# Two attention passes of the differential branch: last block's transposes, reciprocal turns and second pair's first outputs placed behind more products of the next branch

## The reference

```python
def _diff_blocked(q, k, v, lam, scale):
    ...
    def body(qi):                       # 4 blocks of 128 queries
        sc = jnp.einsum('bqkgcd,bskcd->cbkgqs', qi, k).astype(jnp.float32) * scale
        p = jax.nn.softmax(sc, axis=-1)
        w = (p[0] - lam * p[1]).astype(v.dtype)
        return jnp.einsum('bkgqs,bskd->bqkgd', w, v)
...
o_d = (_rmsnorm(o_d, subln_d[l]) * (1.0 - lam_init)).reshape(b, s, NQ_D * 2 * DIFF_DIM)
mix = jnp.concatenate([o_a * jax.nn.silu(g_a), o_b * jax.nn.silu(g_b),
                       o_c * jax.nn.silu(g_c), o_d * jax.nn.silu(g_d)], axis=-1)
x = x + jnp.einsum('bsm,md->bsd', mix, w_out[l])
```

## Time and profile before

| | us |
|---|---|
| median of 3 runs | 1462.36 |
| lowest, highest | 1458.74, 1462.77 |
| the profiled execution, its own time | 1460.76 |
| span of the profiled execution, first to last instruction | 1459.0 |
| TensorE busy in that span | 1398.9 |
| VectorE busy | 851.3 |
| ScalarE busy | 729.0 |
| GpSimd busy | 379.9 |

### The profile page before, as it was taken

How to read it: one execution, slowest core, us unless ns; L and a number is a source line. 1 busy time by engine, 2 the same in 40 slices (tenths; PEclk the granted TensorE clock), 3 DMA queues, 4 the chain that set the end, 5 groups by cost and what they waited for, 6 DMA issues and landing times.

```text
span 1459.0 us, 20170 instructions
## 1 busy us (share of the span) xinstructions
PE 1398.9 (96%) x7530; PEld 1054.9 (72%) x7530; DVE 851.3 (58%) x1505; ACT 729.0 (50%) x1557; POOL 379.9 (26%) x273
## 2 busy tenths in 40 slices
PE   8999999999999999999999899999899999999897
PEld 7867677778787667777777776766667876676666
DVE  4565436367662654364576774548665575558655
ACT  4555447555244554465564364435544464446443
POOL 2232132245231321223464121321102111421001
PEclk9999999999999999999999999999999999999999
DMA  7413451225242131211256523511233341611311
GB/s 234 116 31 92 112 141 29 68 71 224 101 159 59 37 97 51 79 47 50 71 209 195 137 61 71 117 64 51 62 105 87 102 101 29 123 58 51 109 59 58
DMA packets 185894, 135.65 MB, mean 93 GB/s; under 512 B 91334, under 2 KB 166726, under 8 KB 185798
## 3 DMA queue, kind: packets, MB, share of 16 engines
q1 hardware_dynamic: 182022, 120.22, 30.4%
q10 hardware_dynamic: 3776, 14.16, 2.6%
HBM read 122.03 MB, written 12.32 MB: 92 GB/s over the span
## 4 chain that ended last, share of the span: by engine, by line
PE 77%; DVE 12%; ACT 7%; issue 2%; DMA 0%; POOL 0%; ACTq 0%; DVEq 0%; POOLq 0%
PE pb L1576 20%; PE pb L1578 18%; PE pb L1577 18%; PE pb L1598 6%; PE pb L1661 6%; PE pb L1637 4%; ACT prob L1717 3%; ACT tmp L1717 2%; DVE prob L2337 2%; DVE wl L2086 2%; PE pb L1692 1%; ACT wh L1737 1%; PE pb L1609 1%; PE pb L1646 1%; DVE small L2323 1%
## 5 line engine op out<-in xcount | busy, mean ns | idle before, releaser
L2481 POOL TENSOR_TENSOR wl<-wr,wh 128x512 fp32r<-128x512 f32 x178 | 250.7, 1408 | 840.2 <-ACT wh L1737 836.9
L1576 PE MATMUL pb<-xh,wl 128*128 128x512 f32 (+1 forms) x880 | 353.6, 402 | 9.2 <-DVE wl L2086 6.9
L1578 PE MATMUL pb<-xh,wh 128*128 128x512 f32 (+1 forms) x880 | 326.1, 371 | 0.0
L1577 PE MATMUL pb<-xl,wh 128*128 128x512 f32 (+1 forms) x880 | 325.8, 370 | 0.0
L2086 DVE TENSOR_TENSOR wl<-wr,wh 128x512 fp32r<-128x512 f32 x208 | 161.0, 777 | 184.8 <-ACT wh L1737 184.5
L1737 ACT CAST wh<-wr 128x512 fp32r<-128x512 f32 (+1 forms) x386 | 220.4, 606 | 36.8 <-PE pb L1578 17.8
L1576 PEld LDWEIGHTS pb<-xh,wl 128*128 128x128 f32 x880 | 167.8, 191 | 71.2 <-issue 39.8
L1578 PEld LDWEIGHTS pb<-xh,wh 128*128 128x128 f32 x880 | 168.0, 191 | 29.5
L1577 PEld LDWEIGHTS pb<-xl,wh 128*128 128x128 f32 x880 | 168.7, 192 | 22.1 <-issue 3.4
L1717 ACT ACTIVATE prob<-prob,small 128x512 f32<-128x512 f32 (+3 forms) x128 | 76.2, 596 | 119.3 <-DVE small L2300 119.1
L1637 PEld LDWEIGHTS pb<-cst,prob 128*128 128x128 f32 x768 | 91.1, 140 | 50.0 <-issue 30.2
(11 more groups left out here) (198 smaller groups left out, 2350.8 us busy)
## 6 DMA issues: line engine op xcount, KB each, us to landing
wr<-w_in SPq DMA_DIRECT2D x39, 1024.0 KB, 5.4
wr<-w_out SPq DMA_DIRECT2D x14, 1024.0 KB, 5.1
wr<-w_in SPq DMA_DIRECT2D x48, 256.0 KB, 4.5
wr<-w_branch SPq DMA_DIRECT2D x48, 128.0 KB, 2.3
x<-prob SPq DMA_DIRECT2D x12, 512.0 KB, 3.0
wr<-w_mem_kv SPq DMA_DIRECT2D x4, 1024.0 KB, 5.6
prob<-x ACTq DMA_DIRECT2D x2, 2048.0 KB, 11.1
wr<-w_out SPq DMA_DIRECT2D x16, 256.0 KB, 4.2
```

Source lines behind the costliest of these rows:

```text
L1576: e.matmul(ps, ll, rh, start=start, stop=False)
L1577: e.matmul(ps, lh, rl, start=False, stop=False)
L1578: t = e.matmul(ps, lh, rh, start=False, stop=stop)
L2481: t = e.tensor_tensor(wl[:, j % 2, c0:c1], wr[:, j % 2, c0:c1], wh[:, j % 2, c0:c1].bitcast(F32), ALU.subtract)
```

## The change

Three due times are moved, all of them for `D` alone. The reciprocals' turn (`rturn`) of each pair comes 1400 ns of the planner's clock after the last transposes, no longer at once. The first `pv` of the second pair comes 1500 ns later. The transposes of the second pair's last block may come 3500 ns later (10500 after the scores, no longer 7000).

```diff
-FRONTS, FIRST_EXP = 5000, 2800
+FRONTS, FIRST_EXP, LAST_MIX = 5000, 2800, 3500
@@ attention(), back
             if i == 3 and br != "sb":
-                yield 0
+                yield now() + 1400 if br == "D" else 0
                 b = AT.take()
                 put("rturn", l=l, br=br, c=c, b=b, rt=rt[c], u=us[0])
@@ attention(), outputs
             yield copied
             if i == 1:
+                if c and br == "D":
+                    yield now() + 1500
                 ob[c] = OB.take()
@@ attention(), loop over the blocks
-                ready = now() + EXPS.get(br, 4000)
+                ready = now() + EXPS.get(br, 4000) + LAST_MIX * (br == "D" and c == 1 and i == 3)
```

## The result

The changed kernel takes 1466.85 us (median of 7 runs, 1465.52 to 1470.73), the kernel before, beside it, 1461.59 us (7 runs, 1458.74 to 1463.26). The ratio is 1.0042, 95% interval 1.003 to 1.0054: slower by 0.42%; it is the ratio on record and not the quotient of the two medians, which is 1.0036. The forecast was 1467.4 us in a range from 1460.0 to 1472.0.

The account below looks back on a forecast made before the run. TensorE, busy 1398.9 of 1459.0 us, was taken as the bound. Waits gave +0.5 us and clock falls +4.5, together +5.0: 1467.4 us from the median of 1462.36, range 1460.0 to 1472.0.

Parts of the forecast that it names:

- Step 1: The first pair's `rturn` moves behind one more product: an estimated 0.5 us a pass gained, no more.
- Step 2: Second pair's first `pv` and block 3's turns: old waits go, new ones of 1.4 and 2.4 us come; about 0.6 gained.
- E: Start of the first exponential of the second pair's block 3, forecast to come later by some 0.6 us.
- Step 3: Tail and start of `C`: a new 2.8 us wait for VectorE's low part, before the third product behind `C`'s second scores.
- Step 4: In `C`, the 0.54 us wait for a low part that GpSimd delays goes: 0.5 us a pass gained.
- The sum: Both passes without the clock: second pass +1.2 us, first pass -0.7, together +0.5.
- The clock: Behind the long new waits, four places in two passes: three falls to 1.2 GHz at 1.5 us, +4.5 us.
- (a): Rival: the waits come, the clock mostly holds, at most two falls; -0.5 to +3.5 us, about 1463.8; chance 0.27.
- (b): Rival: fill banks free when needed, tail not late, the change wins; up to -12 us, more likely half, 1456; chance 0.12.
- (c): Rival: tail later still, each `dsplit` another us late, a fall at each place; +8 to +10 us, 1471; chance 0.08.

Follow-up runs that it names:

- e1_turn: Kernel before with only the `rturn` edit (1400 later, both pairs): 1459.31 us, ratio 0.9988.
- e10_all_short: Kernel after (all three edits) with 1500 for 3500 in the shift of the second pair's block 3 turns: 1456.76 us, ratio 0.9958 to before.
- e3_mix: Kernel before with only the third edit, the second pair's block 3 turns 3500 later: 1459.67 us, ratio 0.9983.
- e6_turn_mix: Kernel after without the edit of the second pair's first `pv`, so `rturn` and the 3500 shift together: 1468.19 us, ratio 1.0036 to before.
- e5_swap: Kernel after with the copies of `C`'s four value tiles exchanged between ScalarE and VectorE: 1459.56 us, ratio 0.9989 to before.
- e7_turn_mix_short: Kernel before with the `rturn` edit and the block 3 turns shifted by 1500 for 3500, without the `pv` edit: 1456.10 us, ratio 0.9956.
- e12_all_2500: Kernel after (all three edits) with 2500 for 3500 in the shift of block 3's turns: 1458.68 us, ratio 0.9973 to before.
- e2_pv: Kernel before with only the second edit, the second pair's first `pv` 1500 later: 1466.38 us, ratio 1.0025.
- e4_turn_pv: Kernel before with the `rturn` and first `pv` edits, without the shift of block 3's turns: 1464.78 us, ratio 1.0023.
- e9_mix_short: Kernel before with only the third edit, at 1500 for 3500: 1455.63 us, ratio 0.9954.
- e11_short_ahead: e7_turn_mix_short with block 3's mix and reciprocals written out directly behind its scores: 1455.76 us, ratio 0.9955 to before.

## Why the prediction was right, and where it was not

**What bounds the kernel.** Held. In the fourteen kernels a pass differs mostly by what TensorE waits and by the falls; in every pass without a fall its busy time is 98.3 to 99.4 us.

**Step 1, `rturn`, 0.5 us a pass gained.** Not held: from the first marker to block 3's scores the second pass takes 21.61 us before, 21.60 in e1_turn and 21.62 in the kernel after. Nor did it gain further on: e1_turn has 6.41 us of waits where the second pass before has 6.26, since the moved `rturn` pulls a weight piece forward whose GpSimd part lies over `dnewton`. With the clock level in both, e1_turn's pass 2 is 0.52 shorter all the same, all of it busy time.

**Step 2.** Held. E comes 6.55 us behind block 3's scores (1363.21 - 1356.66), 6.09 before: 0.46 where I had 0.6. The keys' bank comes at E + 3.83 (E + 3.7), with a wait of 1.27 (1.4); tile 0's at E + 9.17 (E + 9.2), with 2.21 (2.4). The rule of the Trainium skill, page SBUF — State Buffer, section Who interferes with whom, that VectorE is held up by GpSimd with both its inputs in SBUF and not with one of them in PSUM, is borne out where before only the mixes spoke. GpSimd runs from 1359.88 for 1.29 us, and the instruction of `dnewton` with both inputs in SBUF takes 1.62, 0.69 before. In the second pair's tail GpSimd runs from 1388.23: the instruction with an input in PSUM, beside it nearly all its length, takes 0.68 as alone, and the one behind it, with both in SBUF, 1.14.

```profile
1359.88 1.29 POOL L2483 TENSOR_TENSOR wl<-wr,wh 128x512 fp32r<-128x512 f32 x1 [9.30 <-ACT wh L1739]
1360.10 1.62 DVE L2055 SCALAR_TENSOR_TENSOR scr<-scr,tmp 128x512 f32<-128x512 f32 x1
...
1388.23 1.29 POOL L2483 TENSOR_TENSOR wl<-wr,wh 128x512 fp32r<-128x512 f32 x1 [18.28 <-ACT wh L1739]
1388.21 0.68 DVE L2052 SCALAR_TENSOR_TENSOR scr<-pb,tmp 128x512 f32<-128x512 f32 x1
1388.93 1.14 DVE L2055 SCALAR_TENSOR_TENSOR scr<-scr,tmp 128x512 f32<-128x512 f32 x1
```

**Step 3, the tail.** From the second `pv` (V) to the third product behind `C`'s second scores: V + 17.04 in the first pass after (1071.33 - 1054.29), forecast V + 17.2. e10_all_short has 17.02 and e3_mix 17.09, and the other kernels with a wait there 16.8 to 17.2, but for the second pass of e6_turn_mix with 18.6, where the DMA issues of the last section come in: this chain is about 17 us whatever TensorE does in it. The wait in it was 2.12, forecast 2.8, because TensorE's own work in it is 14.9 us, not 14.4. To the third product, the second pass is longer by 1.2 us once its fall is taken out, where -1.1 + 2.8 = 1.7 was forecast. The first pass is 59.81 us to there, before 60.86: with its own fall only just beginning it is 1.1 shorter, where 0.2 was forecast.

**Step 4 failed.** I took 0.5 us off each pass since the 0.54 in `C` would go, and took the rest of `C` as unchanged. The 0.54 did go, but with 3500 and the other edits the list of `C` itself is another: products have changed places with turns, one of them waits 0.78 for a bank that VectorE's addition (L2426) must free, and from the third product to the second marker TensorE needs 47.9 us (e5_swap, e6_turn_mix, no fall), where it is 46.6 before and 46.7 to 46.8 in e3_mix, e7_turn_mix_short, e10_all_short and e12_all_2500. That is +1.3 a pass where I had -0.5. Of the 1.3, 0.2 is waits; the other 1.1 is busy time with the same instructions. The timelines say where it lies: from start to start, without the waits, the matmuls of the 32 products of this stretch take 23.8 us before and 25.0 in e5_swap, and all else differs by 0.1 in sum. A product's first matmul takes 0.31 to 0.34 us to the next when attention's matmuls stand ahead of it, and mostly 0.22 to 0.24 otherwise, and the order has 30 changes between products and attention where before has 22. But e3_mix and e12_all_2500 have 28, and their products take only 24.2; what else in the order counts stays open.

**The sum.** Without the clock the two stretches are 7.49 - 3 x 1.54 = 2.9 us longer, forecast +0.5; the term that was mis-sized is step 4, by 1.8 us in the second pass and 1.9 in the first, and the stretch up to the third product was 0.5 and 0.9 too dear. **The clock**: three falls of four places at 1.5, forecast and seen, 1.54 measured. The total of +5.0 stands against +5.3 of the medians and +9.1 of the profiled executions. That the number lies so close is luck: the sum without the clock was 2.4 too small, and 2.9 + 4.6 = 7.5 is more than the medians show. How many falls the median run has is not seen in any profile; its granted clock of 0.991, against 0.988 in the profiled execution, speaks for fewer, though falls outside the two passes count in it too. The first pass of before has a fall in its profiled execution; whether in each of its runs, neither.

**The rivals.** (a) had two falls at most and is not what the profile shows. (b) decided, as written, at whether the mix of block 3 ends before TensorE has done tile 1: it did not (the mix ends at 1371.3, tile 1 at 1372.38 - 2.21 = 1370.2). e10_all_short (0.42% faster) and e5_swap (0.11%) show that a win was to be had, by another size or another engine for one copy. (c), each `dsplit` another us late, did not come: 13.5 us behind V where 13.65 was forecast.

## What to carry to other kernels

Moving independent work in front of a wait gained here only where the next wait did not grow by as much. A chain runs from block 3's scores over the mix to the turns, and a second one of 17 us from the last `pv` to the next branch's weights; every product put ahead of the turns is missing behind the `pv`. Count the products on either side against both chains: 15 or 16 between block 3's scores and its turns and 17 to 19 behind the `pv` was right, 21 and 12 (the kernel after) was not, and the size of the shift (1500 or 3500) decided more than whether the other two edits stood beside it. A copy that frees a bank should not stand at the end of the busiest queue: giving it to the other engine took 7 us off, of which 3 are two falls fewer in the profiles; reordering the queue took off 0.3 of the 2.2 us wait and nothing that the time shows.

## What the runs showed of the hardware that I had not expected

The same list with the same waits falls to 1.2 GHz in one pass and not in the other: 1.79 us busy in 4, twice, one fall. In all kernels, the wait of 2.12 in `C` was followed by a fall in six of eight passes, and the wait of 1.8 to 2.2 for tile 0's copy in two of six; the longer ones of e2_pv (2.7 and 1.9 to 2.3, one behind the other) and e4_turn_pv (3.21) in four of four. Waits split into pieces of 1.5 us and less were followed by no fall in e1_turn, e3_mix, e7_turn_mix_short, e9_mix_short, e10_all_short, e11_short_ahead and e12_all_2500. They are no guarantee: in the first pass of before, pieces of 1.2 us and less were followed by one, the only fall in the 16 passes of these eight kernels.

ScalarE's four DMA issues of `accload` take 1.8 to 2.7 us in every pass but one, and what stands behind them on ScalarE is late by it. In e6_turn_mix, second pass, they took 3.65 us and TensorE then waited 1.28 us for the logarithms' input, which it did in no other kernel by more than 0.6. ScalarE, then TensorE:

```profile
1376.69 3.65 ACTq L2017 DMA_DIRECT2D setA<-x  x4
1380.44 0.72 ACT L1717 ACTIVATE tmp<-scr,cst 128x512 f32<-128x512 f32 x1 [8.34 <-issue]
```
```profile
1381.31 1.10 PE L1700 MATMUL pb<-tmp,cst 128*128 128x512 f32 x2 [1.28 <-ACT tmp L1717]
```
